# Two planned row-tile queues, host-packed weights, conv and branch work in later stages, own layer-norm buffers: one decoder layer on eight cores

## What is computed

```python
shift, scale, gate = jnp.split(mod, 3, axis=-1)          # mod = c @ w_ada + b_ada
u = layer_norm(x) * (1.0 + scale[:, None]) + shift[:, None]
proj = jnp.einsum('bsd,de->bse', u, w_in)
q, k, v, z_a, bg, cg, xin, z_c = jnp.split(proj, IN_SPLITS, axis=-1)
...
    s = jnp.einsum('bhiqd,bhikd->bhiqk', q_blk, k).astype(jnp.float32)
    s = s + bias[None, :, None]                          # T5 buckets; causal mask follows
    p = jax.nn.softmax(s, axis=-1)
    a = p[:, :, 0] - lam * p[:, :, 1]
    return jnp.einsum('bhqk,bhkd->bhqd', a.astype(v.dtype), v)
...
y_attn = o.reshape(...) * jax.nn.silu(z_a)               # o: rms-normed per head
y_conv = short_conv(bg, cg, xin, conv_w) * jax.nn.silu(z_c)
g_a, g_c = jnp.split(jax.nn.sigmoid(jnp.einsum('bsd,de->bse', u, w_gate) + b_gate), 2, axis=-1)
merged = (g_a * jnp.einsum('bse,ed->bsd', y_attn, w_branch[0])
          + g_c * jnp.einsum('bse,ed->bsd', y_conv, w_branch[1]))
out = jnp.einsum('bsd,de->bse', merged, w_out)
return layer_norm(DEEPNORM_ALPHA * x + (1.0 + gate[:, None]) * out, ln_gain, ln_bias)
```

## Time and profile before

| | |
|---|---|
| time, median of 3 runs | 4673.52 us (4647.52 to 4820.26) |
| the profiled execution's own time | 4642.81 us |
| its span on the slowest core | 4641.2 us (all cores: 4628.9 to 4641.2) |
| TensorE busy | 4158.3 us, 90% |
| VectorE busy | 2566.1 us, 55% |
| ScalarE busy | 2577.5 us, 56%, of which exp 2073.3 us |
| mean granted TensorE clock | 0.93 |
| moved by DMA | 622.54 MB, mean 134 GB/s |

### The profile page before, as it was taken

How to read it: one execution, slowest core, us unless ns; L and a number is a source line. 1 busy time by engine, 2 the same in 40 slices (tenths; PEclk the granted TensorE clock), 3 DMA queues, 4 the chain that set the end, 5 groups by cost and what they waited for, 6 DMA issues and landing times.

```text
span 4641.2 us, 103947 instructions; the slowest of 8 cores (4628.9 to 4641.2 us)
## 1 busy us (share of the span) xinstructions
PE 4158.3 (90%) x31812; PEld 2373.2 (51%) x31812; DVE 2566.1 (55%) x4622; ACT 2577.5 (56%) x3076; POOL 560.2 (12%) x842
## 2 busy tenths in 40 slices
PE   7168999998399988999999999989999899999997
PEld 2035455555145644565456555544555455555555
DVE  1225355564327572467646576652666736766774
ACT  0015366563046653565766655564777767787761
POOL 0122113222100021001100010111000210000000
PEclk7588899999699988999999999989999999999998
DMA  6785437797534453344543444453343633343433
GB/s 126 156 205 157 131 121 135 131 161 157 159 111 125 143 165 101 121 137 157 150 128 112 141 157 130 157 144 105 116 124 114 180 112 112 112 124 103 137 91 117
DMA packets 376562, 622.54 MB, mean 134 GB/s; under 512 B 171879, under 2 KB 198759, under 8 KB 373992
## 3 DMA queue, kind: packets, MB, share of 16 engines
q1 hardware_dynamic: 267512, 494.47, 35.7%
q0 software_dynamic: 108528, 121.41, 12.1%
HBM read 504.73 MB, written 121.37 MB: 135 GB/s over the span
## 4 chain that ended last, share of the span: by engine, by line
PE 78%; DMA 7%; issue 5%; ACT 3%; DVE 3%; SPq 2%; POOL 1%; DVEq 0%; ACTq 0%; another core or an unknown queue 0%; POOLq 0%
PE psa L696 78%; DMA xn_scr<-xn 3%; ACT PB L1105 3%; SPq L879 2%; DMA fp_scr<-xn 1%; DMA uX<-xn_scr 1%; DMA xr<-x_all 1%; DMA uA<-xn_scr 1%; DVE TTr L653 0%; DMA v_scr<-vsb 0%; POOL rs L653 0%; DVE xn L662 0%; DMA W<-w_ada 0%; DMA W<-w_out 0%; DVE st L864 0%
## 5 line engine op out<-in xcount | busy, mean ns | idle before, releaser
L1105 ACT ACTIVATE PB<-psa 128x1024 bf16<-128x1024 f32 x2112 | 2073.3, 1026 | 762.2 <-PE psa L696 643.8
L696 PE MATMUL psa<-PB,KV 64*128 64x512 bf16 (+3 forms) x9216 | 2176.1, 367 | 79.1 <-DVE PB L653 20.7
L696 PE MATMUL psa<-uC,W 64*128 64x512 bf16 x7168 | 1380.4, 382 | 9.8 <-DVE sz L1015 1.3
L696 PE MATMUL psa<-QT,KV 64*128 64x512 bf16 (+3 forms) x4608 | 1247.7, 367 | 61.9 <-ACT PB L1105 45.2
L653 DVE TENSOR_TENSOR TTr<-PB 128x1024 bf16<-128x1024 bf16 (+1 forms) x1024 | 682.6, 671 | 770.2 <-ACT PB L1105 756.2
L696 PEld LDWEIGHTS psa<-PB,KV 64*128 64x128 bf16 x9216 | 775.8, 96 | 629.8 <-issue 437.5
L696 PEld LDWEIGHTS psa<-uC,W 64*128 64x128 bf16 x7168 | 583.9, 95 | 323.9 <-issue 107.3
L696 PEld LDWEIGHTS psa<-QT,KV 64*128 64x128 bf16 x4608 | 382.3, 96 | 380.2 <-issue 275.1
L696 PE MATMUL psa<-uA,W 64*128 64x512 bf16 x2048 | 369.9, 395 | 172.1 <-DVE uA L662 123.8
L730 ACT ACTIVATE ksb<-psa 128x512 bf16<-128x512 f32 x192 | 112.6, 597 | 515.3 <-PE psa L696 469.7
L653 DVE TENSOR_TENSOR TTr<-TTr 128x1024 bf16<-128x1024 bf16 (+1 forms) x512 | 326.8, 638 | 33.4 <-DVE TTr L653 1.8
(11 more groups left out here) (97 smaller groups left out, 3438.1 us busy)
## 6 DMA issues: line engine op xcount, KB each, us to landing
W<-w_scr SPq DMA_DIRECT2D x364, 512.0 KB, 4.6
KV<-kT_scr SPq DMA_DIRECT2D x288, 256.0 KB, 3.0
KV<-v_scr SPq DMA_DIRECT2D x288, 256.0 KB, 3.1
xr<-x_all SPq DMA_DIRECT2D x96, 512.0 KB, 4.7
w_scr<-W SPq DMA_DIRECT2D x52, 512.0 KB, 5.8
xn_scr<-xn POOLq DMA_DIRECT2D x64, 256.0 KB, 4.9
kT_scr<-ksb POOLq DMA_DIRECT2D x128, 128.0 KB, 2.8
v_scr<-vsb POOLq DMA_DIRECT2D x32, 512.0 KB, 4.7
```

The lines of the kernel that those rows point to most:

```text
L696: return e.matmul(mk_out(b), l_, r_, start=st, stop=True, skip_group_check=True)
L1105: ex = g.add("act", lambda e, pb=pb, sap=sap: e.activation(pb[:], sap, AF.Exp), key - dk - 1.0, 0.921, [], [pb[:]])
```

## The change

- **Planner.** Each row tile has its own time at which it is free; the lowest key among a free tile's ready matmuls is issued, a pair is no longer needed. Latencies are given by engine, and larger.
- **Prologue.** A0's layer norm gets the lowest keys. Each piece of w_ada (now [6, 8, 128, 512], contiguous) has an own home in buffers that are still unused (YC, YA, uC0, KV, QS, TTr). `fps` moves from `xn` to a part of MT. Small loads that are needed late may not be planned before 180 us (`T_LATE`).
- **Weights.** The host packs all 26 units as [26, 2, 128, 2048]: a half is one DMA with 8 KB in a row for each partition.
- **Buffers.** Layer norm has own rings `xl` (2), `stl`, `mvl`, `rsl` (3 each); D has `xo` (2). `vsb` has 2 buffers instead of 1, `ft` 4 instead of 5. The bias table is stored to DRAM (`tab_scr`) and loaded for each head (ring of 2).
- **Stages.** 0: A1; 1: A2; 2: A3 C0; 3: D0 A4 C1; 4: D1 C2 A5 D2; 5: C3 D3 A6; 6: C4 D4 A7 C5; 7: D5 C6 D6 C7; tail D7. A's layer norm has the key `base`.
- **Convolution.** The job of B of one block is emitted after the C job of the next block.

```diff
-SLOT = 0.2163
-LAT = 0.12
-LATPE = 0.2
-HAND = 0.3
+SLOT = 0.2163
+LAT = {"act": 0.2, "dve": 0.1, "pool": 0.15, "sp": 0.1, PE0: 0.27, PE8: 0.27}
+HAND = 0.33
+T_LATE = 180.0
...
-            t = end + lat
-            if op.eng in (PE0, PE8) and s.eng in (PE0, PE8):
-                t = end
-            elif op.eng == s.eng and not op.dma:
-                t = end + 0.06
+            if s.eng in (PE0, PE8):
+                t = end if op.eng in (PE0, PE8) else t + 0.045
...
-        tp = max(pe_t, pe_next)
+        tp = max(min(tile_free.values()), t_issue, pe_next)
...
+            for e in sorted(tile_free, key=lambda e_: tile_free[e_]):
+                if tile_free[e] > t + 1e-9:
...
+                for bk_, hp in pe_av[e].items():
...
+                    if got is None or hp[0][0] < got[0]:
+                        got = (hp[0][0], e, bk_)
...
-            d = max(x.dur for x in chosen if x is not None)
-            end = t + d
...
+            end = t + x.dur
...
+            tile_free[e] = end
+            t_issue = t + 0.005
...
-        TAB = sb("TAB", [128, NH, 384], BF16)
+        TABr = ring("TAB", 2, [128, 384], BF16)
...
-        xr = ring("xr", 3, [128, D])
+        xr = ring("xl", 2, [128, D])
+        xor_ = ring("xo", 2, [128, D])
...
-        vsbr = ring("vsb", 1, [128, 4, 4, 128], BF16)
+        vsbr = ring("vsb", 2, [128, 4, 4, 128], BF16)
...
-        ftr = ring("ft", 5, [128, 512])
+        ftr = ring("ft", 4, [128, 512])
...
+        stl = ring("stl", 3, [128, 12])
+        mvl = ring("mvl", 3, [128, 2])
+        rsl = ring("rsl", 3, [128, 1])
...
-            for q in range(4):
-                w = Wr()
...
+            for k in range(8):
+                w = homes()
+                dma("sp", key - 5 + k * 0.5, w, w_ada[ch, k], t0=t0)
+                job_mm(j, key + k * 0.5, crep_v[:, k, :], w, dur=SLOT * 4)
...
-        fps = xnr()
+        fps = MT[:, 4:6, :].rearrange("p a n -> p (a n)")
...
-                    for src, c0, o0, n in units[name]:
-                        dma("pool", key + hf, wv_[:, :, o0:o0 + n],
-                            src[hf * 512:(hf + 1) * 512, c0:c0 + n].rearrange("(k p) c -> p k c", p=128),
-                            nb=128 * 4 * n * 4)
+                    dma("pool", key + hf, w[:], w_pack[ui, hf], nb=128 * 2048 * 4)
...
+            tab = TABr()
+            dma("sp", key0 - 20, tab[:], tab_scr[h], reads=[("tab", h)])
...
-        emit_A(0, kA, -180.0)
+        emit_A(0, kA, -302.0)
...
+            text = "A1|A2|A3 C0|D0 A4 C1|D1 C2 A5 D2|C3 D3 A6|C4 D4 A7 C5|D5 C6 D6 C7|D7"
...
-                    emit_A(t, fk, base + ln_ * 0.2)
+                    emit_A(t, fk, base)
```

More of the change, by code:

```diff
@@ L79, in add @@
         op.idx = len(self.ops)
-        op.ready, op.end, op.order, op.done = 0.0, 0.0, -1, False
+        op.ready, op.end, op.order, op.done = t0, 0.0, -1, False
         op.need, op.sem, op.val, op.prev = False, None, None, 0
@@ L274, in finish_reader @@
             bank_lastreaders[j.bank].append(op)
-            bank_free[j.bank] = max(bank_free[j.bank], end + LAT)
+            bank_free[j.bank] = max(bank_free[j.bank], end + LAT[op.eng] + 0.045)
             if j.rleft == 0:
@@ L304, in schedule @@
                 heapq.heappush(pe_av[op.eng].setdefault(bank_of(op), []), (op.key, seq[0], op))
-            f0 = set()
-            f8 = set()
             nh = None
-            for bk_ in allbanks:
-                for fb, other, own in ((f0, PE8, PE0), (f8, PE0, PE8)):
+            got = None
+            for e in sorted(tile_free, key=lambda e_: tile_free[e_]):
+                if tile_free[e] > t + 1e-9:
+                    if any(pe_av[e].values()):
+                        nh = tile_free[e] if nh is None else min(nh, tile_free[e])
+                    continue
+                other = PE8 if e == PE0 else PE0
+                for bk_, hp in pe_av[e].items():
+                    if not hp:
+                        continue
@@ L339, in schedule @@
-            chosen = [a, b]
-            if a is None and b is None:
+                        nh = x.end + HAND if nh is None else min(nh, x.end + HAND)
+                        continue
+                    if got is None or hp[0][0] < got[0]:
+                        got = (hp[0][0], e, bk_)
+                if got is not None:
+                    break
+            if got is None:
                 cand = []
@@ L356, in schedule @@
                 continue
-            d = max(x.dur for x in chosen if x is not None)
-            end = t + d
[L359 to L372, removed]
-                if gk is not None:
-                    first = gk not in grp_begun
-                    grp_begun.add(gk)
-                    x.n = (1 if first else 0)
-                ndone += 1
-                complete(x, end)
-            pe_t = end
-            pe_next = end
+            _, e, bk_ = got
+            x = heapq.heappop(pe_av[e][bk_])[2]
+            end = t + x.dur
+            x.order = len(order["pe"])
+            order["pe"].append(x)
+            x.end = end
+            y = last_on[PE8 if e == PE0 else PE0].get(bk_)
+            if y is not None:
+                x.deps[y] = 3
+            gk = x.job if x.job is not None else x.grp
+            if gk is not None:
+                first = gk not in grp_begun
+                grp_begun.add(gk)
+                x.n = (1 if first else 0)
+            last_on[e][bk_] = x
+            ndone += 1
+            complete(x, end)
+            tile_free[e] = end
+            t_issue = t + 0.005
+            pe_next = 0.0
             continue
@@ L506, in __init__, with pack_weights, pick @@
             block.sync(mk("sp"))
+UNITS = ([(k, cn) for cn in range(2) for k in "kvqzo"] + [("c", cb) for cb in range(8)] + [("g", cb) for cb in range(8)])
+def pack_weights(w_in, w_gate, w_branch, w_out):
+    def pick(name, i):
+        base = {"q": 0, "k": 1024, "v": 2048, "z": 3072}
+        if name in base:
+            return w_in[:, base[name] + i * 512:base[name] + (i + 1) * 512]
+        if name == "o":
+            return w_out[:, i * 512:(i + 1) * 512]
+        cs = slice(i * 128, (i + 1) * 128)
+        if name == "c":
+            return np.concatenate([w_in[:, 4096 + n * 1024:5120 + n * 1024][:, cs] for n in range(4)], 1)
+        return np.concatenate([w_gate[:, :1024][:, cs], w_gate[:, 1024:][:, cs], w_branch[0][:, cs], w_branch[1][:, cs]], 1)
+    out = np.empty((len(UNITS), 2, 128, 2048), np.float32)
+    for u, (name, i) in enumerate(UNITS):
+        out[u] = pick(name, i).reshape(2, 4, 128, 512).transpose(0, 2, 1, 3).reshape(2, 128, 2048)
+    return out
 def build_nc(NJ=8, **kw):
@@ L1043, in emit_D @@
                     if cn == 0:
-                        dma("sp", key - 15, x_[:], x_all[r0:r0 + 128, :])
+                        dma("sp", key - 15, x_[:], x_all[r0:r0 + 128, :], t0=T_LATE)
                     tm = ftr()
```

180 lines of the change are left out of this document (72 added, 108 removed).

## The result

The changed kernel takes 4200.32 us (median of 4 runs, 4197.49 to 4208.81), 0.9016 [0.8967, 0.9064] of the kernel before measured beside it: faster by a tenth. The forecast was 4065 us, with a range of 3780 to 4310; the likeliest case's own range was 3940 to 4180. Runs in which one die had a lower granted clock are left out of the ratios, and where a profile fell in such a run (e_shared, e_best) its numbers here are those of core 1, on the other die.

A forecast was written before the change was run, and what follows sets the result against it. Thin A phases behind D's stores, the prologue and starts above the steady pace were taken as the bounds. Terms -148 - 16 - 10 - 244 + 40 - 200 = -578 us took about 4641 us to 4065, range 3780 to 4310.

The forecast's parts named there:

- the thin stretches: Five A phases with few matmul starts, 326 us excess; own norm buffers and A at stage start should give -244 us.
- added waits: Moved norms in DVE's in-order queue amid attention, ahead of work that frees PB buffers: +40 us (0 to +120).
- no 100 us without exponentials: Sign for the thin stretches: no stretch that long without ScalarE's exponentials should remain.
- The pace: Matmul starts after the prologue, 0.016 us each above the steady pace; two queues and new latencies should give -200 us.
- Clean stretches at about 0.118 us a start: Sign for the pace: long stretches without thin phases, at 0.124 us per matmul start before, should reach about 0.118.
- The prologue: Time before attention: first score matmul at 205 us against 353, -148 us (bounds -209 to -53).
- 105 us between 69 and the 165 of before: Prologue, A0's projections: time taken between 69 us at the matmul pace and 165 us before, as weights' loads remain.
- Stages 0 and 1: Stretch from 350 to 766 us, excess 63 us; half of the 33 us not due to float32 gate records goes: -16 us.
- Packing: Conv and branch weights in 2 issues per unit instead of 8; stretch of first use gains -10 us (0 to -14).
- A: Rival, the pace stays: one PE queue in program order, so two planned queues gain nothing; 4265 us, chance 0.20.
- C: Rival, thin stretches move: the norm's chain on Pool, SP and DVE stops attention inside stages; 4289 us, chance 0.16.
- D: Rival, slower: weight loads come late through the same five W buffers; 4772 us at 1.7 us each, chance 0.03.

The follow-up runs named there:

- e_shared: Changed kernel with layer norm and D sharing one ring of three x buffers and the statistics rings again: 4326.63 us, without a ratio; core 1 4275.7 us.
- e_best: Changed kernel with table copies from DRAM, float32 modulation matmuls planned at twice the time, five `ft` and three `ksb` buffers: 0.8986 of the kernel before.
- e_plan: Kernel before with only the planner changed (own time per row tile, new latencies and durations): 4599.16 us, 0.9889 of the kernel before.
- e_pair: Changed kernel with the planner of before (locked pairs, old latencies and durations): 4290.58 us, 0.921 of the kernel before.
- e_oldlat: Changed kernel with two planned queues kept, but the old latencies, hand-over and durations: 4295.9 us, 0.9219 of the kernel before.
- e_f32: Changed kernel with the modulation's float32 half matmuls reckoned at twice the time in the plan: 4165.18 us, 0.8949 of the kernel before.
- e_fpfast: Changed kernel with the position table's rows stored once to DRAM and copied from there, not from one SBUF partition: 4158.27 us, 0.8943 of the kernel before.
- e_gate: Changed kernel with group j's layer-norm load of x waiting until group j-2's projections stored their last q: 4206.93 us, 0.9053 of the kernel before.
- e_unpack: Changed kernel with the 52 first loads of projection, convolution and branch weights from the four original arrays, modulation still packed: 0.9026 of the kernel before.
- e_fp: Changed kernel with the position table's stores and copies put after A0's eight layer-norm stores: 4203.61 us, 0.9039 of the kernel before.

## Why the prediction was right and where it was wrong

**Faster, and mainly by the thin stretches: right.** "The five thin stretches should then run near the clean pace" was put at -244 with +40 for added waits; with both it measured -287, 83 us more than forecast. Norms of A3 to A7 come before D's end, as said. The other sign, "no 100 us without exponentials", failed narrowly: one stretch of 105 us is left, before stage 4. The sharing was the named cause, and e_shared shows that it holds norms back; but its own price is some 80 us, and the old stage order's 38. The planner is not it: alone it leaves the stretches (e_plan, 253 us), and without it only 62 us without exponentials stand before stage 4 (e_pair). Neither the buffers nor the order alone brings the 287 back; as I read it the two cover for each other. No run undoes just these two together.

**The pace: right in size, and half right in cause.** "Clean stretches at about 0.118 us a start" came out as 0.1187. Per start the gain was 0.0056 us of 0.0064 forecast. But the forecast gave it to the planner. "The corrected latencies alone remove planned-too-early operands" holds inside the changed kernel (e_oldlat); on the kernel before, the planner brings stage 7 from 0.125 to between 0.123 and 0.126 (e_plan), and without it the changed kernel already has 0.122 (e_pair). The other half came with the rest of the change, which the term did not count. In us it is -126 and not -200, since I had counted all 31,040 starts, and the stretches outside the clean ones have other limits. That the sum of the thin stretches and the pace came out near its forecast is luck.

**The prologue: wrong by 91 us.** First scores at 294 us, not 205. Scale and shift were there at 88.6 of 90. Two steps failed. "Eight layer-norm tiles at 6 to 7 us end by 65, beside it": the earlier trace rows gave the 6 us, but the tiles stood in DVE's order behind the modulation's evacuations (e_f32: 20 us of first score), and their stores behind the table's copies (e_fpfast: 39 us). I had read the fp_scr wait as a matter of the shared buffer and costed its removal by moving the buffer; the transfer itself was the cost. And "105 us between 69 and the 165 of before" for A0: with the copies out of the way it took 115 to 255, 140 us, and in e_best 87 to 261, with weight loads and evacuations ending PE's waits.

**Stages 0 and 1: wrong in sign.** I gave -16, and it measured +27. What I had costed with "These norms now stand in DVE's queue amid attention", spread over seven norms, falls largely into these two stages, because half of the norms run there (32 stores of `xn` between 294 and 754 us). e_gate takes 32 us of it away. It was inside the bounds of that term (0 to +120), but in another place. Put off, it is paid in stages 2 and 3 (e_gate), so the place was wrong and the price was not avoidable that way.

**The tail: left out.** "One `ft` buffer less I cost at nothing" was the failed step: +15 us, of which e_best gets 10 back with five `ft`. The expectation that blamed the planner for it (e_pair) was wrong too.

**Packing: the amount was right, -10 to -16, and the cause wrong.** e_unpack shows none.

**The rivals.** A's number (4265) lies nearer to the result than the forecast, but for another reason: the pace did not stay, and the missing time stands in the prologue and the first stages. Of A's mechanism the runs bear out what it says of the queues. C (chains of the norm stop attention inside stages) is what stages 0 and 1 show in small. D did not come: clean stretches run denser on the same five W buffers.

## What to carry to other kernels

A wait that names a buffer may be the wait for the transfer that fills or empties it: before costing its removal, look at what that transfer takes and what else its queue and the DMA engines carry then. Work that is made free to run early runs as early as it can, and lands on the stage with the least cover; price the added waits there. And a planner that orders in-order engines gained here from true latencies, more than from a second queue, and only once other waits were out of its way.

## What was not expected of the hardware

- Eight DMAs that each copy one SBUF partition's 1.5 KB 128 times to DRAM land after 32 us (median; 56 in e_fp), and from a row in DRAM after 9.9. While they ran, three quarters of all DMA engine time went to 1.5 MB in 50 us, and another queue was held: eight transposes took 63.09 us of SP in e_fp instead of 10.82.
- A DMA transpose of 512 x 128 in bf16 holds SP's queue for 1.3 to 1.6 us, a plain load for 0.3 to 0.7 (rows above, 292 to 327 us).
- Float32 records of 512 columns in the prologue ran at three speeds, all at a granted clock of 1.00: with one row tile 8 in 7.03 us, with both in turn 8 in 3.59 us at first, and some 5 us later 29 in 6 us, 0.21 each, half of what the forecast took as a floor. What changed in between no run shows. Timeline of PE, and the stretch 58 to 64:

```profile
29.88 7.03 PE L698 MATMUL psa<-YA,MT 64*128 64x512 f32 x8
...
53.41 3.59 PE L698 MATMUL psa<-KV,MT 64*128 64x512 f32 x8
```

```profile
58.00:64.00 6.00, 6.00 (x29) 3.50 (x28) 0.00 (x0) 0.00 (x0) 0.00 (x0) 1.00 0.48 194
```
